# A fourth buffer for the broadcast rows of a state-space loop, and one weight block loaded after the loop instead of before it

## What is computed

```python
cs = jnp.cumsum(dtc * A, axis=2)                     # cumulated logs, one row per head
decay_ls = jnp.exp(jnp.where(causal, cst[..., :, None] - cst[..., None, :], -jnp.inf))
cb = jnp.einsum('bclgn,bcsgn->bcgls', cf, bf)
m = cb[:, :, :, None] * decay_ls * jnp.moveaxis(dtc, 2, -1)[..., None, :]
y = jnp.einsum('bcgels,bcsgep->bclgep', m, xf)
states = jnp.einsum('bclgn,bclge,bclgep->bcgepn', bf, decay_end * dtc, xf)
h_last, h_prev = lax.scan(step, h0, (chunk_decay, states))
y = y + jnp.einsum('bclgn,bcgepn,bclge->bclgep', cf, h_prev, jnp.exp(cs))
y = y.reshape(Bn, L, SSD_INNER) * jax.nn.silu(z.astype(F32))   # z: the gate, a product of x and a weight
```

## Time and profile before

| what | value |
|---|---|
| median of 3 runs | 2442.16 us (2440.03 to 2445.89) |
| the profiled execution, its own time | 2438.43 us |
| its span | 2436.6 us |
| TensorE busy | 2168.1 us, 89% of the span |
| VectorE busy | 1227.0 us, 50% |
| ScalarE busy | 897.4 us, 37% |
| mean granted clock of TensorE, share of full | 0.941 |
| the state-space loop, first scan to first gate product | 1193 to 1389 us |

### The profile page before, as it was taken

One profiled execution on the slowest core, in us unless ns is written; L12 is line 12 of the kernel. 1 busy time (PEld: TensorE's weight loads), 2 busy tenths in 40 slices (PEclk: granted clock), 3 DMA queues, 4 the chain that ended last, 5 costly groups with the idle time before them and its releaser, 6 DMA issues.

```text
span 2436.6 us, 36238 instructions
## 1 busy us (share of the span) xinstructions
PE 2168.1 (89%) x14582; PEld 1974.9 (81%) x14582; DVE 1227.0 (50%) x1678; ACT 897.4 (37%) x1362; POOL 172.9 (7%) x248
## 2 busy tenths in 40 slices
PE   7998879799999997998587899994899999999990
PEld 5776657699999987997566798984899999999990
DVE  1334531433233325665687857223566756666664
ACT  0033420421112114333335445113454655565553
POOL 2011210000000000000143200002000000000001
PEclk9999989899999998999698899996899999999995
DMA  4236770932133111221355322233476677576765
GB/s 140 69 109 190 221 212 23 392 87 96 53 87 96 52 53 35 86 86 54 104 156 177 106 76 69 81 110 104 160 247 209 231 231 246 197 254 218 239 211 168
DMA packets 298958, 349.32 MB, mean 143 GB/s; under 512 B 10951, under 2 KB 253911, under 8 KB 298795
## 3 DMA queue, kind: packets, MB, share of 16 engines
q1 hardware_dynamic: 285574, 299.67, 39.2%
q0 software_dynamic: 12768, 47.49, 5.2%
q10 hardware_dynamic: 504, 0.60, 0.1%
HBM read 299.87 MB, written 47.85 MB: 143 GB/s over the span
## 4 chain that ended last, share of the span: by engine, by line
PE 82%; DVE 8%; ACT 4%; DMA 3%; issue 2%; POOL 1%; SPq 0%; POOLq 0%; DVEq 0%; ACTq 0%
PE ps L1090 18%; PE ps L1381 10%; PE ps L839 9%; PE ps L1363 9%; PE ps L1107 8%; PE ps L1272 8%; PE ps L1365 6%; PE ps L1366 1%; DMA ring<-cs_rows 1%; PE ps L858 1%; PE ps L853 1%; PE ps L1175 1%; PE ps L941 1%; PE ps L1025 1%; ACT xT L1440 1%
## 5 line engine op out<-in xcount | busy, mean ns | idle before, releaser
L1363 PE MATMUL ps<-xgs,blk_hi 128*128 128x384 f32 x1232 | 245.8, 338 | 2.8 <-DVE xgs L2414 2.8
L2076 DVE TENSOR_TENSOR fw_l<-ring,fw_h 128x1024 fp32r<-128x1024 f32 (+1 forms) x60 | 79.7, 1332 | 287.6 <-ACT fw_h L1579 287.6
L1363 PEld LDWEIGHTS ps<-xgs,blk_hi 128*128 128x128 f32 x1232 | 220.6, 189 | 3.5 <-issue 3.0
L1579 ACT ACTIVATE fw_h<-ring 128x1024 fp32r<-128x1024 f32 (+1 forms) x60 | 68.7, 1149 | 399.2 <-PE ps L1090 335.7
L2409 DVE TENSOR_TENSOR blk_lo<-arena,blk_hi 128x2048 fp32r<-128x2048 f32 (+1 forms) x98 | 197.7, 2024 | 32.6 <-ACT blk_hi L1762 32.6
L1381 PE MATMUL ps<-blk_hi,hs 128*128 128x512 f32 x704 | 193.6, 393 | 0.0
L1365 PEld LDWEIGHTS ps<-xgs,blk_lo 128*128 128x128 f32 x1408 | 182.5, 192 | 0.0
L1365 PE MATMUL ps<-xgs,blk_lo 128*128 128x192 f32 x1408 | 182.4, 271 | 0.0
L1762 ACT ACTIVATE blk_hi<-arena 128x2048 fp32r<-128x2048 f32 (+1 forms) x98 | 165.6, 1702 | 32.4 <-DMA arena<-in_moe_w 32.4
L839 PE MATMUL ps<-xT,ring 128*128 128x288 f32 (+1 forms) x672 | 168.3, 414 | 9.2 <-issue 6.5
L839 PEld LDWEIGHTS ps<-xT,ring 128*128 128x128 f32 (+1 forms) x672 | 126.8, 189 | 49.4 <-issue 9.0
(11 more groups left out here) (471 smaller groups left out, 3973.8 us busy)
## 6 DMA issues: line engine op xcount, KB each, us to landing
arena<-in_moe_w SPq DMA_DIRECT2D x76, 1024.0 KB, 5.4
ring<-in_moe_w SPq DMA_DIRECT2D x50, 1024.0 KB, 5.3
ring<-in_ssd_w_in SPq DMA_DIRECT2D x48, 512.0 KB, 4.6
ring<-in_ffn_w SPq DMA_DIRECT2D x44, 512.0 KB, 5.2
ring<-in_cache_k SPq DMA_DIRECT2D x64, 256.0 KB, 3.0
arena<-in_cache_v SPq DMA_DIRECT2D x48, 256.0 KB, 3.0
arena<-in_moe_w SPq DMA_DIRECT2D x24, 512.0 KB, 4.0
sorted_x<-ring POOLq DMA_DIRECT2D x1, 10752.0 KB, 34.4
```

Of the source, the lines that this page charges most:

```text
L1363: mmul(o[:, 0:2 * CAP], wh[:, k, :], xgs[:, k, :, :].rearrange("p u n -> p (u n)"), start=(k == 0), stop=False)
L1579: f(fw_h[:, n % RAW, 0:K, :], ring[:, m % RAW, 0:K, (n % 2) * P:(n % 2 + 1) * P], ACT.Copy).then_inc(w_hi, 1)
L2076: tt(fw_l[:, n % RAW, 0:K, :], ring[:, m % RAW, 0:K, (n % 2) * P:(n % 2 + 1) * P], fw_h[:, n % RAW, 0:K, :].bitcast(F32), ALU.subtract).th ...
```

## The change

The rows get a fourth buffer: `eb[3]` takes the first 1152 floats of slot 0 and `ex[3]` the 576 behind them, which is where gate block 1 was loaded. Tile t now uses buffer t % 4. Three tiles' rows are asked for before the loop instead of two, and inside it the two places that asked for t+2 and t+3 ask for t+3 and t+4. Block 1 of the gate is no longer loaded before the loop but at the head of the loads behind it. So that one more semaphore is free, `in_hist` is merged into `in_par`, and `row_mm` and `row_up` continue `xt_mm` and `xt_up`.

```diff
-        eb = [spare(0, 2048 + 1152 * n, 2, T) for n in range(3)]
-        ex = [spare(0, 5504 + 576 * n, T) for n in range(3)]
+        eb = [spare(0, 2048 + 1152 * n, 2, T) for n in range(3)] + [spare(0, 0, 2, T)]
+        ex = [spare(0, 5504 + 576 * n, T) for n in range(3)] + [spare(0, 1152, T)]
...
-            for n in range(2):
-                load(C_Z + n, 0, pair(w, 0, KD, n * CW))
+            load(C_Z, 0, pair(w, 0, KD, 0))
...
             def cs_load(t):
-                n = t % 3
+                n = t % 4
...
             sp.wait_ge(cs_out, 32)
-            cs_load(0)
-            cs_load(1)
+            for t in range(3):
+                cs_load(t)
             for t in range(3):
                 h0_load(t)
             for g in range(SG):
                 t0 = 2 * g
                 sp.wait_ge(y_ok, t0)
-                if t0 + 2 < XT:
-                    cs_load(t0 + 2)
+                if t0 + 3 < XT:
+                    cs_load(t0 + 3)
                 sp.wait_ge(fs_up, g + 1)
...
-                if t0 + 3 < XT:
+                if t0 + 4 < XT:
                     sp.wait_ge(y_ok, t0 + 1)
-                    cs_load(t0 + 3)
+                    cs_load(t0 + 4)
                 h0_store(t0)
                 h0_store(t0 + 1)
             sp.wait_ge(ss_out, 16 * XT)
             sp.wait_ge(y_ok, XT)
             w6 = I["ssd_w_out"][0]
-            for m in range(2, NZ + KD):
+            for m in range(1, NZ + KD):
                 j, h = (m - NZ) // 2, (m - NZ) % 2
-                sp.wait_ge(w_lo, LO0 + z_last(m - 2) + 1)
+                if m >= 2:
+                    sp.wait_ge(w_lo, LO0 + z_last(m - 2) + 1)
...
-            sp.wait_ge(row_up, 9)
+            sp.wait_ge(xt_up, 19)
...
-            pe.wait_ge(in_par, 16 * 12)
-            pe.wait_ge(in_hist, 48)
+            pe.wait_ge(in_par, 16 * 15)
```

More of the change, by code:

```diff
@@ L327, in build @@
         used = sem("used")
-        in_x, in_par, in_hist = sem("in_x"), sem("in_par"), sem("in_hist")
+        in_x, in_par = sem("in_x"), sem("in_par")
         in_gatew, in_small, in_pages = sem("in_gatew"), sem("in_small"), sem("in_pages")
@@ L362, in build @@
         PRE_UP = dict(x0=1, small=2, x1=3, cb=4)
-        cs_out, cs_in, bq_ok = sem("cs_out"), [sem(f"cs_in{n}") for n in range(3)], sem("bq_ok")
+        cs_out, cs_in, bq_ok = sem("cs_out"), [sem(f"cs_in{n}") for n in range(4)], sem("bq_ok")
         h0_in_s, h0_tr, h0_up, hd_ok = [sem(f"h0_in{n}") for n in range(3)], sem("h0_tr"), sem("h0_up"), sem("hd_ok")
@@ L369, in build @@
         z_gate, z_sqd, z_sum, z_rt, z_ok = [sem(n) for n in ("z_gate", "z_sqd", "z_sum", "z_rt", "z_ok")]
-        row_mm, row_up, tl_out = sem("row_mm"), sem("row_up"), sem("tl_out")
+        tl_out = sem("tl_out")
         xt_mm, xt_up, sc_out = sem("xt_mm"), sem("xt_up"), sem("sc_out")
@@ L1200, in within @@
                         o = ps[64 * hh:64 * hh + 64, q, c * P:(c + 1) * P] if c < NCH else ps[64 * hh:64 * hh + 64, q + 1, 0:NS]
-                        mmul(o, x_dt[g % 2][:, c, hc:hc + 64], eb[t % 3][:, hh, c * P:min(c * P + P, T)], start=True, stop=True)
+                        mmul(o, x_dt[g % 2][:, c, hc:hc + 64], eb[t % 4][:, hh, c * P:min(c * P + P, T)], start=True, stop=True)
             def from_h0(t):
@@ L1329, in _ @@
                 if n >= 4:
-                    pe.wait_ge(row_up, n - 3)
+                    pe.wait_ge(xt_up, 10 + n - 3)
                 for q in range(4):
@@ L1336, in _ @@
                         last = tr(ps[0:36, n % 4, q * P:(q + 1) * P], lru_tail[:, q, :], ident[:])
-                last.then_inc(row_mm, 1)
-            pe.wait_ge(row_up, 9)
+                last.then_inc(xt_mm, 1)
+            pe.wait_ge(xt_up, 19)
             def sorted_in(r):
@@ L1418, in _ @@
                 ld(par_in[lo:lo + 4, 2, :], I[name][0].rearrange("(t h) d -> t (h d)", h=2)).then_inc(in_par, 16)
-            ld(h0_in[0:DEC_B, :], I["state_lru_h"][0]).then_inc(in_hist, 16)
-            ld(lhist_in[0:DEC_B * HIST, :], I["state_lru_conv"][0].rearrange("b t d -> (b t) d")).then_inc(in_hist, 16)
-            ld(shist_in[0:DEC_B * HIST, :], I["state_ssd_conv"][0].rearrange("b t d -> (b t) d")).then_inc(in_hist, 16)
+            ld(h0_in[0:DEC_B, :], I["state_lru_h"][0]).then_inc(in_par, 16)
+            ld(lhist_in[0:DEC_B * HIST, :], I["state_lru_conv"][0].rearrange("b t d -> (b t) d")).then_inc(in_par, 16)
+            ld(shist_in[0:DEC_B * HIST, :], I["state_ssd_conv"][0].rearrange("b t d -> (b t) d")).then_inc(in_par, 16)
             def banks(b):
@@ L1650, in exps @@
             def exps(t):
-                e = eb[t % 3]
-                act.wait_ge(cs_in[t % 3], 48 * (t // 3 + 1))
+                e = eb[t % 4]
+                act.wait_ge(cs_in[t % 4], 48 * (t // 4 + 1))
                 for hh in range(2):
@@ L1749, in _ @@
             for n in range(9):
-                act.wait_ge(row_mm, n + 1)
+                act.wait_ge(xt_mm, 10 + n + 1)
                 if n < 8:
-                    f(tail_s[0:27, n * 512:(n + 1) * 512], ps[0:27, n % 4, :], ACT.Copy).then_inc(row_up, 1)
+                    f(tail_s[0:27, n * 512:(n + 1) * 512], ps[0:27, n % 4, :], ACT.Copy).then_inc(xt_up, 1)
                 else:
-                    f(tail_l[0:36, :], ps[0:36, n % 4, :], ACT.Copy).then_inc(row_up, 1)
+                    f(tail_l[0:36, :], ps[0:36, n % 4, :], ACT.Copy).then_inc(xt_up, 1)
             def width(b):
@@ L2255, in y_out_tile @@
                 dve.wait_ge(yt_mm, t + 1)
-                dve.wait_ge(cs_in[t % 3], 48 * (t // 3 + 1))
+                dve.wait_ge(cs_in[t % 4], 48 * (t // 4 + 1))
                 dve.wait_ge(y_ok, t)
                 y = ps[:, q:q + 2, :].rearrange("p b n -> p (b n)")
-                link(tt(y_in_t[:], y[:, T:T + 448], ex[t % 3][:, P:T], ALU.mult))
+                link(tt(y_in_t[:], y[:, T:T + 448], ex[t % 4][:, P:T], ALU.mult))
                 link(stt(xbc[:, t, :], xbc[:, t, :], d_exp[:, t:t + 1], y[:, 0:T], ALU.mult, ALU.add))
@@ L2458, in _ @@
             sm, nm, vs, sd, rs, nr_ = [stat[:, 8 * n:8 * n + 5] for n in range(6)]
-            dve.wait_ge(in_par, 16 * 14)
+            dve.wait_ge(in_par, 16 * 17)
             def scaled_rows(c):
```

## The result

The changed kernel takes 2420.72 us (median of 4 runs, 2419.36 to 2422.0), the kernel before 2444.02 in the runs beside it (2440.03 to 2449.91): the ratio is 0.9903, 95% interval 0.988 to 0.9925. That is 23.3 us or 1.0% faster, against 13.6 forecast; the time lies inside the range of 2419 to 2438.

What follows compares the result with a forecast made beforehand. Loop iterations were taken as bound by rows requested only after a sample-state store landed, delaying state products and DVE. Gain 21.9 minus 8.3 for slow products, others 0: 13.6 us off 2442.16, giving 2428.5; range 2419 to 2438.

Steps and rivals of the forecast that it cites:

- Term 1: State-space loop: waits for rows go, six iterations fall from 147.72 to 125.8 us, 21.9 us less.
- ACT's remaining wait: ACT still waits for the odd tile's rows, about 2 us per iteration, 3.7 at most, 14 in all, costing nothing.
- cover: Slack between the end of ACT's odd-tile exponentials and its next needed work, L1665: 1 to 3 us.
- Term 2: TensorE's clock in the loop: three state products stay slow, 2.78 us each, taking 8.3 us off the gain.
- rival A: TensorE's clock holds, none or one slow state product: gain 19.1 to 21.9 us, time 2420 to 2423; chance 0.18.
- the forecast's own case: Two to four slow state products in the six loop iterations, gain 10.8 to 16.3 us; chance 0.50.
- Term 3: Loop start: a third broadcast delays the states 3.1 us, at least 1.95 covered by TensorE's wait for DVE; cost 0.
- Term 4: After the loop: second gate block lands later, hidden by TensorE's first two tiles; cost 0, otherwise 5 to 8 us.
- Rivals B: Five or six slow state products in the loop: gain 5.2 to 8.0 us, time 2434 to 2437; chance 0.20.
- C: The wait moves: odd tile's rows land too late, delaying ACT's L1665; time 2437 to 2442; chance 0.09.
- D: Slower: the second gate block, after the loop, becomes the new bound; time 2447 or more; chance 0.03.

Runs made afterwards that it cites:

- e7: Changed kernel with the odd tile's rows asked for later, both requests of an iteration at the middle place; 2426.1 us, ratio 0.9928.
- e5: Kernel before with TensorE's pause filled by doing the four transposes ahead of it four times instead of once; 2442.8 us, ratio 0.9998.
- e9: Kernel before with its old requests; only ACT's list changed, copying B to b_tok before the even tile's exponentials; 2442.8 us, ratio 0.9979.
- e1: Kernel before with gate block 1 loaded after the loop and nothing else changed; 2445.6 us, ratio 1.000.
- e2: Changed kernel with its fourth buffer, but each tile's rows asked for where the kernel before asked for them; 2442.9 us, ratio 0.9991.
- e3: Kernel before with three buffers and early gate block; only the even tile's row request moved ahead of the second sample store; 2423.1 us, ratio 0.9919.
- e4: Changed kernel run once more without an edit, with its own profile; 2420.4 us, ratio 0.9907.
- e10: Changed kernel with only DVE's small decay product of the odd tile moved behind the even tile's y_out_tile; 2415.8 us, ratio 0.9873.
- e12: e3 with the small decay product of the odd tile also moved behind y_out_tile; 2421.7 us, ratio 0.991.
- e8: Changed kernel with both of DVE's decay products of the odd tile moved behind pre_small; 2437.6 us, ratio 0.9975.
- e6: Changed kernel with TensorE's pause filled by repeated transposes, four times instead of once; 2419.4 us, ratio 0.9908.
- e11: e10 with TensorE's pause filled by repeated transposes, four times instead of once; 2417.8 us, ratio 0.9882.

## Why the prediction was right, and what was mis-sized

- **Term 1 (21.9 us)** came out as worked out. The iteration of 18.88 + 2.09 = 20.97 us stood in the trace of before, in pieces of different iterations, and is the one that the changed kernel repeats. ACT's remaining wait is 16.6 us for the 14 given, the longest 4.4 for the 3.7 given, and costs nothing. Its cover can be read from the trace after: behind these exponentials ACT sat idle for 0.5 to 3.4 us before its first L1664 of the next iteration, where I had said 1 to 3. e7 bears this out only roughly, since it put the rows off by about 1 us, not 2.5.
- **Term 2 (minus 8.3 us)** failed, in the count and in the price. The step was that two of the three falls of the clock came from the pause before L1215, since they began before the wait for `b_tok`, and that the count of three would stay. The changed kernel has one slow product of six, twice. It costs 1.06 us (3.05 instead of 1.99) and no collision follows, so 1.1 us instead of 8.3, where I had charged 2.78 for each. With that, the sum is 21.9 - 1.1 = 20.8, which is what the six iterations show. The order in time that I read was right, but it did not show that these products would stay slow without the wait: e5, with the pause filled, had four slow products; e9, with the pause but without the wait for `b_tok`, had none. Open is why the pause was followed by a fall more often in the old loop: in the profiles of before, e1 and e2 the clock fell soon after it, ahead of the wait for `b_tok`, 6 times in 18 iterations; in the seven profiles with the pause and without that wait (the changed kernel, e3, e4, e7, e9, e10, e12) 5 times in 42. The case that came was rival A, one slow product, to which I gave 0.18; the forecast's own case, two to four, with its 0.50, did not. The time, 1.7 us above the lower end of the range, lies inside because the range took in A's case as well. Of the Trainium skill, "TensorE: Matmul & The Clock Gate", the section on waits for transfers between bursts ("HAM oscillation — how this bites in real kernels") fits e5, and e9 too, where the clock fell at the waits for L1665, behind which stands ACT's wait for the rows; what the section "A second HAM failure mode: psum-queue depth-cycling" says of short pauses shows in one product of six in the changed kernel, and in all six of e8.
- **Against which time.** The measured gain, 23.3 us, is above even the 21.9 that I gave as the most. The other 2.5 us between 20.8 and 23.3 are not explained by an experiment; the interval of the ratio alone holds gains of 18 to 29 us. Most likely they are the old loop's spread. Its six iterations took 147.7 us in the profile that I worked from, 151.3 and 149.9 in e1 and e2, whose loops wait for the rows in the same way. I subtracted from the shortest of three. The four runs of before beside the result spread over 9.9 us, those of the changed kernel over 2.6. Whether this comes from waiting for transfers is not shown: e8, where ACT waits as little for the rows as in the changed kernel (17.6 us), spread over 12.7.
- **Term 3 (0)** was right: the first state products still waited 1.95 us for DVE, no more. They start 0.6 us later (1189.89), but the whole stage does, from before the broadcasts.
- **Term 4 (0)** was right: issued at 1371.92, in use at 1377.34, needed at 1386.59; e1 measures the whole edit at 1.000, within 3.7 us.
- **Rivals B, C and D** did not occur. C's mechanism exists: e7 brought it about in one iteration of six.

## What to carry to other kernels

When an engine waits for a load, look first at what stands ahead of the load in the issuing engine's list: here one request behind a store's landing cost about 0.8% of the whole kernel, and moving it gave most of the gain without a new buffer. To predict an iteration without a wait, add up the stretches of the bounding engine from iterations in which they were undisturbed, and take the time of before from several profiles: three of the same waits gave 147.7, 149.9 and 151.3 us here. Don't charge a fall of TensorE's clock to the pause that happens to precede it while a longer wait follows: test one without the other, and look where the wait went.

## What was not expected of the hardware

The rank of pauses: of the 42 iterations of the changed kernel (two profiles), e3, e7, e9, e10 and e12, all with a pause of 1.8 to 2.1 us, five ended with a state product at the lower clock; with the pause filled to 0.7 or 0.8 us (e6, e11) none of 12 did, and with 3.1 us (e8) six of six. e8 differs in more than the pause, so this is an order seen, not a cause shown. And collisions with GpSimd move rather than vanish: L767 was paid for by L2233, L2216, L2213 or the cast L2212, at 1.0 to 1.7 us, wherever DVE's list stood at that moment.
